# Gate matrix of a PEER layer: the last row of each group on ScalarE, three buffers, merge two groups behind

## The chip, the cores and the metric

The kernel runs on one core of a Trainium2 chip. The time is that of one execution on the device, in microseconds (us); lower is better. Three runs of the kernel before took 3328.36, 3329.63 and 3330.40 us.

## What is computed

Two blocks with 256 tokens of width 2048: first an S5 mixer and a sparse attention, then a HGRN2 and gated delta mixer followed by a PEER feed-forward layer. Only the PEER layer matters here. It has 16384 experts, written as pairs (i, j) of two indices of 128. Each token has 8 heads, and each head takes its 16 best experts, so a token has 128 entries (index i, index j, gate):

```python
best, pos = lax.top_k(cand, P_TOPK)
expert = i1[pos // P_TOPK] * N_KEYS + i2[pos % P_TOPK]
gate = jax.nn.softmax(best, axis=-1)
hid = gelu(x . u_tab[expert])
y = sum(gate * hid * v_tab[expert])
```

The kernel gathers nothing. It multiplies every token with all experts and weighs the result with a gate matrix that holds 0 for the experts that a token did not choose. For token t, that matrix is a 128 x 128 product of two matrices with one nonzero in each of the token's 128 entries: R (entry x first index, with the gate there) and C (entry x second index, with a 1 there): W[t] = R^T C.

## The kernel before

All weights stream through the core in pieces of 512 KB: SyncE issues the transfer into a ring of three raw slots; ScalarE rounds the piece into its high part (`high`, L231, 128x1024); VectorE subtracts to get the low part (`low`, L237, 128x1024); TensorE multiplies high and low parts (24 matmuls for a piece in `up_piece`, L2373). A slot comes free for the next transfer when its `low` is done.

The experts are 64 pairs of 256 (`up(j)`, four pieces of the first table, and `down(j)`, four pieces of the second, L2439). In `peer` the first LEAD = 16 `up`s come before the first `down`. Eleven of them (STORED) have their gelu put into the large tile `w` before the gates are known; five (HELD) are computed in the course of the gate loop and keep their gelu in PSUM banks 2, 3, 4, 5 and 0 (`HELD_BANK`). So the loop that makes the gate matrix also carries 20 pieces of `up`.

**The gate loop** goes over 64 groups of 4 tokens (`GATE_GROUPS`, `PER_GROUP`). Its engines run their own programs in order and meet at semaphores:

- VectorE, for group n: four rows (L2657, `tensor_scalar` is_equal and mult over the iota with the token's first index and gate as per-partition operands, 128x128 each); the four columns in one instruction (L2660, 128x512); `merge(n - 1)` (L2647, 128x88: the product's cells of the 11 stored pairs times the stored gelu); in 20 of the 64 groups (`early_slot`: 0, 4, 7, 10, 13, 16, 20 ... 61) one `low`. The rows and columns have two buffers, so that group n waits for the product of group n - 2.
- TensorE: in the 20 slots first one held piece (L2373, 24 matmuls), then `gates(n)` (L2414): four matmuls of 128x128 in fp32, each of which the profile shows as two records, into PSUM bank 6 or 7. It waits for the rows, the columns and `placed` of group n - 2.
- ScalarE: in the slots one `high` (L231), five times a gelu (L2485) too; then `place(n)` (L2492, 128x424: the other cells of the product, copied into `w`), which waits for `merged(n)`.
- SyncE: the piece transfers (L2335), each when a `low` is done.

After the loop TensorE runs `up(16)` and then `down(0)`. In `up(16)` (bank 16 % 3 = 1) it waits for `stored` only, and `down(0)` waits for all of the gates. VectorE multiplies the five held gelus with their gates (L2671), which waits for `placed(63)`. Then a loop over the rest of the pairs follows, in which VectorE also adds up the output (L2685).

`k.stepper(eng, sem)` gives a function that makes its engine wait for the completion of the instruction just issued; it is used where the next instruction reads the result.

Of the kernel before, what the change touches and what calls it, by code (L numbers as in the profile page):

```python
# [25 lines left out]
ACT = mybir.ActivationFunctionType  # L26
AX = mybir.AxisListType

P = 128
# [2176 lines left out]
WG, HN_LOW, YACC = 0, 32768, H3  # L2206
# [7 lines left out]
STORED = LEAD - HELD  # L2214
HELD_BANK = (2, 3, 4, 5, 0)
PER_GROUP = 4
GATE_GROUPS = T // PER_GROUP
E1T, E2T, GT = (YACC + T * i for i in range(3))
GROWS, GCOLS = YACC + 768, YACC + 1792

# [32 lines left out]
def peer(k):  # L2255


    nc, ps = k.nc, k.ps
# [11 lines left out]
    w, w_t = k.at(WG, 32768), k.at(WG, 32768).rearrange("p (i t) -> p t i", t=T)  # L2270
    y = k.at(YACC, 4096)
    e1t, e2t, gt = (k.at(o, T) for o in (E1T, E2T, GT))
    rows = [k.at(GROWS + 512 * b, 512) for b in range(2)]
    cols = [k.at(GCOLS + 512 * b, 512) for b in range(2)]
    gparts = [k.split_small(P + 256 * i - WORK0, 512, 512 * i) for i in range(2)]
    keys_in, copied, sums, raised, e_done, chosen, turned, e_out = (k.sem("pq_" + n) for n in (
        "keys copied sums raised exps chosen turned turned_out").split())
    rows_ready, cols_ready, product, placed, merged = (k.sem("gm_" + n) for n in (
        "rows_ready cols_ready product placed merged").split())
    stored, gelu_done, gated, g_high, g_low, y_full, y_free, reloaded = (k.sem("ex_" + n) for n in (  # L2280
        "stored gelu_done gated g_high g_low y_full y_free rows_reloaded").split())
    E0 = PIECES * AT_EXPERTS
# [11 lines left out]
    def u_piece(j, part):  # L2294

        return E0 + PIECES * (j if j < LEAD else 2 * j - LEAD) + part

    def v_piece(j, part):
        return E0 + PIECES * (LEAD + (2 * j + 1 if j < WITH_UP else WITH_UP + j)) + part
# [7 lines left out]
    def slot_of(j):  # L2307
        return w[:, j * 512:(j + 1) * 512]
# [12 lines left out]
    def early_slot(n):  # L2321


        count = PIECES * HELD
        return n * count // GATE_GROUPS != (n - 1) * count // GATE_GROUPS

    with nc.Block() as block:
# [24 lines left out]
        def _(pe):  # L2352
# [25 lines left out]
            def up(j, m, looped):  # L2378

                if j == LEAD and not looped:  # L2380
                    pe.wait_ge(stored, STORED)
                elif j >= LEAD:
                    pe.wait_ge(gated, m * BODY + (j - 2))
                elif j >= 3:
                    pe.wait_ge(stored, j - 2)
                for part in range(PIECES):
                    up_piece(u_piece(j, part), part, j % 3, m)
# [17 lines left out]
                mm.then_inc(turned, 1)  # L2405

            def gates(n):
                b = n % 2
                pe.wait_ge(rows_ready, n + 1)
                pe.wait_ge(cols_ready, n + 1)  # L2410
                if n >= 2:
                    pe.wait_ge(placed, n - 1)
                for j in range(PER_GROUP):
                    mm = nc.tensor.matmul(ps[:, 6 + b, j * P:(j + 1) * P], rows[b][:, j * P:(j + 1) * P],  # L2414
                                          cols[b][:, j * P:(j + 1) * P], start=True, stop=True)
                mm.then_inc(product, 1)

# [51 lines left out]

        @block.scalar  # L2470
        def _(act):
            early = iter(range(E0, E0 + PIECES * (LEAD + 1)))

            def high(n):
                for _, c in zip(range(n), early):
                    k.high(act, c)

            def copy(h):
                act.wait_ge(sums, h + 1)
                nc.scalar.copy(sc.rearrange("p (t n) -> p t n", t=TT)[:, :, h * 256:(h + 1) * 256],  # L2480
                               ps[:, 3 + h % 5, :].rearrange("p (t n) -> p t n", t=TT)).then_inc(copied, 1)

            def gelu(c, bank, m=0):
                act.wait_ge(k.multiplied, m * PER + (c + 1))
                nc.scalar.activation(ps[:, bank, :], ps[:, bank, :], ACT.Gelu).then_inc(gelu_done, 1)  # L2485

            def held_gelu(i):
                gelu(u_piece(STORED + i, PIECES - 1), HELD_BANK[i])

            def place(n):  # L2490
                act.wait_ge(merged, n + 1)
                nc.scalar.copy(w_t[:, n * PER_GROUP:(n + 1) * PER_GROUP, 2 * STORED:],  # L2492
                               ps[:, 6 + n % 2, :].rearrange("p (j i) -> p j i", i=P)[:, :, 2 * STORED:]
                               ).then_inc(placed, 1)

            def step(j, m, looped):

                if looped or 1 <= j <= WITH_UP:
                    gelu(u_piece(j + LEAD - 1, PIECES - 1), (j + LEAD - 1) % 3, m)
                act.wait_ge(gated, m * BODY + (j + 1))  # L2500
                if looped or j >= 2:

                    act.wait_ge(k.multiplied, m * PER + (v_piece(j - 2, PIECES - 1) + 1))
                nc.scalar.copy(gparts[j % 2][0], w[:, bass.ds(m * (512 * BODY) + j * 512, 512)]).then_inc(g_high, 1)
                if j < WITH_UP:
                    for part in range(PIECES):
                        k.high(act, v_piece(j, part), m, PER)
                if j < PAIRS - 1:
                    for part in range(PIECES):
                        k.high(act, v_piece(j, PIECES) + part, m, PER)  # L2510

            for c in range(PIECES * AT_WQ, PIECES * (AT_WQ + 1)):
                k.high(act, c)
            for h in range(PH):
                if h + 1 < PH:
                    for c in range(PIECES * (AT_WQ + h + 1), PIECES * (AT_WQ + h + 2)):
                        k.high(act, c)
                else:
                    high(PIECES)
                act.wait_ge(k.multiplied, PIECES * (AT_WQ + h + 1))  # L2520
                nc.scalar.copy(qry[:, h * BANK:(h + 1) * BANK], ps[:, (AT_WQ + h) % BANKS, :]).then_inc(k.bank_free, 1)
                if h:
                    copy(h - 1)
            for j in range(STORED):
                high(PIECES)
                act.wait_ge(k.multiplied, u_piece(j, PIECES - 1) + 1)
                nc.scalar.activation(slot_of(j), ps[:, j % 3, :], ACT.Gelu).then_inc(stored, 1)
                if j == 0:
                    copy(PH - 1)
                if j == 6:  # L2530
                    act.wait_ge(raised, 1)
                    nc.scalar.activation(gate, gate, ACT.Exp).then_inc(e_done, 1)
            piece = 0
            high(1)
            for n in range(GATE_GROUPS):
                if early_slot(n):
                    high(1)
                    if piece and piece % PIECES == 0:
                        held_gelu(piece // PIECES - 1)
                    piece += 1  # L2540
                place(n)
            held_gelu(HELD - 1)
            act.wait_ge(k.spilled, 16)
            act.dma_start(y, k.h3_rows).then_inc(reloaded, 16)
            run(act, step)

        @block.vector
        def _(dve):
            v = k.stepper(dve, k.vstep)
            tt_, ts_ = nc.vector.tensor_tensor, nc.vector.tensor_scalar  # L2550
            early = iter(range(E0, E0 + PIECES * (LEAD + 1)))

            def low(n):
                for _, c in zip(range(n), early):
                    k.low(dve, c)
# [88 lines left out]
            def merge(n):  # L2644
                dve.wait_ge(product, n + 1)
                cells = w_t[:, n * PER_GROUP:(n + 1) * PER_GROUP, 0:2 * STORED]
                tt_(cells, ps[:, 6 + n % 2, :].rearrange("p (j i) -> p j i", i=P)[:, :, 0:2 * STORED], cells,  # L2647
                    ALU.mult).then_inc(merged, 1)

            dve.wait_ge(stored, STORED)  # L2650
            for n in range(GATE_GROUPS):
                b = n % 2
                if n >= 2:
                    dve.wait_ge(product, n - 1)
                for j in range(PER_GROUP):
                    t = n * PER_GROUP + j
                    last = ts_(rows[b][:, j * P:(j + 1) * P], k.iota, e1t[:, t:t + 1], gt[:, t:t + 1],  # L2657
                               ALU.is_equal, ALU.mult)
                last.then_inc(rows_ready, 1)
                tt_(cols[b].rearrange("p (j i) -> p j i", i=P), k.iota.unsqueeze(1).to_broadcast([P, PER_GROUP, P]),  # L2660
                    e2t[:, n * PER_GROUP:(n + 1) * PER_GROUP].unsqueeze(2).to_broadcast([P, PER_GROUP, P]),
                    ALU.is_equal).then_inc(cols_ready, 1)
                if n:
                    merge(n - 1)
                if early_slot(n):
                    low(1)
            merge(GATE_GROUPS - 1)
            dve.wait_ge(placed, GATE_GROUPS)
            for i in range(HELD):
# [171 lines left out]
```

## Time and profile before

| | |
|---|---|
| runs | 3328.36, 3329.63, 3330.40 us |
| profiled execution, its own time | 3324.11 us |
| its span | 3322.3 us |
| TensorE busy | 3073.0 us (92%) |
| VectorE busy | 2201.1 us (66%) |
| ScalarE busy | 1431.5 us (43%) |
| GpSimd busy | 29.5 us (1%) |
| mean granted TensorE clock | 0.96 |

The profiled execution has its own time, and a span inside it (first to last instruction). Busy times are sums over the whole span and say nothing of a single stage; the stage of the gate loop has to be cut out by its times. PE is TensorE's matmuls and PEld its weight loads, which overlap; DVE is VectorE, ACT ScalarE. A row of the timeline has the start in us, the time to the end of the (merged) instructions, the engine and line, and in brackets how long the engine had been idle and what ended that. Durations include the latency to the last write; the next instruction of an engine often starts before that, so the distance of two starts (a "step") is what an instruction costs its engine.

### The profile page before, as it was taken

Reading aid. Unit: us, or ns where it says so; the run is one execution under the profiler, and the core shown is the slowest. Engines: PE = TensorE matmul, PEld = TensorE weight load, DVE = VectorE, ACT = ScalarE, POOL = GpSimd, SP = SyncE. Lnnn points to the kernel's source line nnn. Section 1 sums busy time; section 2 is a strip of 40 time slices with the busy share of each in tenths; the row PEclk is TensorE's granted clock in tenths of the full one; section 3 lists DMA queues with packets and bytes.
Section 4 is the critical chain, followed back from the end, with each engine's and each line's share of the span. In section 5 each row is a group of like instructions: output and inputs, shape, how many; then the busy total and the mean of one; then the engine's idle time right before and its main releaser. Section 6 shows DMA issues by size and latency. Waiting matters only on the chain. (4 is left out here: it accounts for less than half of the span.)

```text
span 3322.3 us, 60164 instructions
## 1 busy us (share of the span) xinstructions
PE 3073.0 (92%) x23855; PEld 2521.6 (76%) x23922; DVE 2201.1 (66%) x3106; ACT 1431.5 (43%) x1805; POOL 29.5 (1%) x32
## 2 busy tenths in 40 slices
PE   7787899999987789999979988999999999999997
PEld 6674799988886678998869877777777777777654
DVE  8765534555555675575549999777777777777654
ACT  4223434565652543363434445444444444444443
POOL 0000000000000020000000000000000000000000
PEclk9768899999998899999989999999999999999999
DMA  5214655544434433353645532655565655655664
GB/s 199 77 52 152 204 158 184 161 140 140 140 123 156 140 115 102 109 172 102 196 159 173 174 112 77 212 193 189 192 198 194 191 189 193 197 190 186 194 193 150
DMA packets 143950, 529.74 MB, mean 159 GB/s; under 512 B 16992, under 2 KB 17760, under 8 KB 142048
## 3 DMA queue, kind: packets, MB, share of 16 engines
q1 hardware_dynamic: 140400, 510.33, 47.5%
q10 hardware_dynamic: 3312, 15.92, 1.3%
q8 instruction: 189, 3.10, 0.4%
q14 instruction: 49, 0.40, 0.0%
HBM read 521.99 MB, written 4.19 MB: 158 GB/s over the span
## 5 line engine op out<-in xcount | busy, mean ns | idle before, releaser
L237 DVE TENSOR_TENSOR mem<-mem,rounded 128x1024 bf16<-128x1024 f32 x952 | 1155.2, 1227 | 759.4 <-ACT rounded L231 751.9
L231 ACT CAST rounded<-mem 128x1024 fp32r<-128x1024 f32 x952 | 993.4, 1047 | 1399.6 <-PE ps L264 337.2
L264 PE MATMUL ps<-rounded 128*128 128x256 f32 x3328 | 475.1, 292 | 49.8 <-DVE mem L237 42.5
L264 PEld LDWEIGHTS ps<-rounded 128*128 128x128 f32 x3328 | 423.4, 193 | 55.2 <-issue 24.7
L264 PE MATMUL ps<-rounded,mem 128*128 128x256 bf16 x3328 | 445.2, 279 | 0.0
L264 PE MATMUL ps<-mem,rounded 128*128 128x256 bf16 x3328 | 428.5, 276 | 13.7 <-DVE mem L237 13.7
L264 PEld LDWEIGHTS ps<-mem,rounded 128*128 128x128 bf16 x3328 | 319.3, 99 | 61.2 <-DVE mem L237 9.0
L264 PEld LDWEIGHTS ps<-rounded,mem 128*128 128x128 bf16 x3328 | 316.3, 98 | 61.7 <-issue 1.4
L2439 PE MATMUL ps<-rounded 128*128 128x512 f32 x1024 | 335.5, 441 | 2.7 <-DVE mem L2695 2.1
L2685 DVE TENSOR_TENSOR mem<-mem,ps 128x512 f32<-128x512 f32 x392 | 268.5, 685 | 66.9 <-PE ps L2439 60.0
L2439 PE MATMUL ps<-mem,rounded 128*128 128x512 bf16 x969 | 294.4, 381 | 3.7
L2373 PE MATMUL ps<-rounded 128*128 128x256 f32 x2048 | 287.7, 288 | 8.8 <-DVE mem L2692 2.4
L2373 PE MATMUL ps<-rounded,mem 128*128 128x256 bf16 x2048 | 275.8, 276 | 0.0
L2373 PEld LDWEIGHTS ps<-rounded 128*128 128x128 f32 x2048 | 259.2, 189 | 17.8 <-issue 8.0
L2439 PE MATMUL ps<-rounded,mem 128*128 128x512 bf16 x1016 | 271.1, 387 | 0.5
L2373 PE MATMUL ps<-mem,rounded 128*128 128x256 bf16 x2048 | 246.5, 272 | 1.6 <-DVE mem L237 1.6
L2439 PEld LDWEIGHTS ps<-rounded 128*128 128x128 f32 x1024 | 189.4, 189 | 58.2 <-DVE mem L2695 2.5
L2373 PEld LDWEIGHTS ps<-mem,rounded 128*128 128x128 bf16 x2048 | 199.6, 98 | 27.3 <-DVE mem L237 2.7
L2373 PEld LDWEIGHTS ps<-rounded,mem 128*128 128x128 bf16 x2048 | 186.7, 96 | 36.0
L2439 PEld LDWEIGHTS ps<-rounded,mem 128*128 128x128 bf16 x1024 | 98.9, 97 | 126.5
L2439 PEld LDWEIGHTS ps<-mem,rounded 128*128 128x128 bf16 x1024 | 78.8, 97 | 137.1 <-issue 70.8
L2414 PE MATMUL ps<-mem 128*128 128x128 f32 x512 | 72.1, 285 | 23.5 <-DVE mem L2660 21.7
(407 smaller groups left out, 2368.6 us busy)
## 6 DMA issues: line engine op xcount, KB each, us to landing
mem<-experts SPq DMA_DIRECT2D x512, 512.0 KB, 4.2
mem<-weights SPq DMA_DIRECT2D x440, 512.0 KB, 3.6
mem<-x_t SPq DMA_DIRECT2D x4, 512.0 KB, 9.9
mem<-x_rows SPq DMA_DIRECT2D x1, 2048.0 KB, 7.6
mem<-ln_g ACTq DMA_DIRECT2D x2, 1024.0 KB, 5.2
mem<-ln_b ACTq DMA_DIRECT2D x2, 1024.0 KB, 7.6
mem<-cmp_w_k ACTq DMA_DIRECT2D x4, 512.0 KB, 5.5
mem<-cmp_w_v ACTq DMA_DIRECT2D x4, 512.0 KB, 4.8
```

The source lines that it names most:

```text
L231: self.nc.scalar.copy(self.parts(c % SLOTS)[0], self.raw(c % RAW)).then_inc(self.high_done, 1)
L237: self.nc.vector.tensor_tensor(wl, self.raw(c % RAW), wh.bitcast(F32), ALU.subtract).then_inc(self.low_done, 1)
L264: mm = self.nc.tensor.matmul(self.ps[:, bank, half * 256:half * 256 + 256], a, b, start=(part == 0 and n == 0), stop=(part == PIECES - 1 a ...
L2373: mm = nc.tensor.matmul(ps[:, bank, half * T:half * T + T], a, b, start=(part == 0 and n == 0), stop=(part == PIECES - 1 and n == len(KIND ...
L2414: mm = nc.tensor.matmul(ps[:, 6 + b, j * P:(j + 1) * P], rows[b][:, j * P:(j + 1) * P], cols[b][:, j * P:(j + 1) * P], start=True, stop=True)
L2439: mm = nc.tensor.matmul(ps[:, bank, :], a, b, start=(j <= WITH_UP and half == 0 and i == 2 * tt), stop=((j < WITH_UP or j == PAIRS - 1) an ...
L2685: nc.vector.tensor_tensor(y[:, a:a + BANK], y[:, a:a + BANK], ps[:, bank, :], ALU.add).then_inc(y_free, 1)
```

## The change

`PER_GROUP - 1` rows of a group are still made by VectorE. The last row is made by ScalarE in two instructions, `row(n)`: dist = |e1[t] - iota| (Abs, the index as a per-partition bias), then relu(gate - 2 dist), which is the gate where dist is 0 and 0 elsewhere. The two are joined by a step wait. ScalarE makes the rows of groups 0 and 1 ahead of the loop, and `row(n + 2)` at the head of its group n, before that group's `high`, gelu and `place(n)`. Rows and columns have three buffers, and the product three banks (6, 7, 1), so that the waits for a buffer reach back three groups. VectorE merges group n - 2 in group n, and the last two groups after the loop. TensorE waits for `last_row` as well, and `up(16)`, which uses bank 1, waits for `placed` of 63 groups (that is for `place(62)`, the last user of bank 1).

```diff
--- before.py
+++ after.py
@@ -2216,7 +2216,8 @@
 PER_GROUP = 4
 GATE_GROUPS = T // PER_GROUP
 E1T, E2T, GT = (YACC + T * i for i in range(3))
-GROWS, GCOLS = YACC + 768, YACC + 1792
+GROWS, GCOLS, GDIST = YACC + 768, YACC + 2304, YACC + 3840
+GATE_BANK = (6, 7, 1)
 
 
 
@@ -2270,13 +2271,14 @@
     w, w_t = k.at(WG, 32768), k.at(WG, 32768).rearrange("p (i t) -> p t i", t=T)
     y = k.at(YACC, 4096)
     e1t, e2t, gt = (k.at(o, T) for o in (E1T, E2T, GT))
-    rows = [k.at(GROWS + 512 * b, 512) for b in range(2)]
-    cols = [k.at(GCOLS + 512 * b, 512) for b in range(2)]
+    rows = [k.at(GROWS + 512 * b, 512) for b in range(3)]
+    cols = [k.at(GCOLS + 512 * b, 512) for b in range(3)]
     gparts = [k.split_small(P + 256 * i - WORK0, 512, 512 * i) for i in range(2)]
     keys_in, copied, sums, raised, e_done, chosen, turned, e_out = (k.sem("pq_" + n) for n in (
         "keys copied sums raised exps chosen turned turned_out").split())
-    rows_ready, cols_ready, product, placed, merged = (k.sem("gm_" + n) for n in (
-        "rows_ready cols_ready product placed merged").split())
+    dist = [k.at(GDIST + P * b, P) for b in range(2)]
+    rows_ready, last_row, cols_ready, product, placed, merged = (k.sem("gm_" + n) for n in (
+        "rows_ready last_row_ready cols_ready product placed merged").split())
     stored, gelu_done, gated, g_high, g_low, y_full, y_free, reloaded = (k.sem("ex_" + n) for n in (
         "stored gelu_done gated g_high g_low y_full y_free rows_reloaded").split())
     E0 = PIECES * AT_EXPERTS
@@ -2378,7 +2380,7 @@
             def up(j, m, looped):
 
                 if j == LEAD and not looped:
-                    pe.wait_ge(stored, STORED)
+                    pe.wait_ge(placed, GATE_GROUPS - 1)
                 elif j >= LEAD:
                     pe.wait_ge(gated, m * BODY + (j - 2))
                 elif j >= 3:
@@ -2405,13 +2407,16 @@
                 mm.then_inc(turned, 1)
 
             def gates(n):
-                b = n % 2
+                b = n % 3
                 pe.wait_ge(rows_ready, n + 1)
+                pe.wait_ge(last_row, n + 1)
                 pe.wait_ge(cols_ready, n + 1)
-                if n >= 2:
-                    pe.wait_ge(placed, n - 1)
+                if n == 2:
+                    pe.wait_ge(stored, STORED)
+                if n >= 3:
+                    pe.wait_ge(placed, n - 2)
                 for j in range(PER_GROUP):
-                    mm = nc.tensor.matmul(ps[:, 6 + b, j * P:(j + 1) * P], rows[b][:, j * P:(j + 1) * P],
+                    mm = nc.tensor.matmul(ps[:, GATE_BANK[b], j * P:(j + 1) * P], rows[b][:, j * P:(j + 1) * P],
                                           cols[b][:, j * P:(j + 1) * P], start=True, stop=True)
                 mm.then_inc(product, 1)
 
@@ -2469,6 +2474,7 @@
 
         @block.scalar
         def _(act):
+            a = k.stepper(act, k.astep)
             early = iter(range(E0, E0 + PIECES * (LEAD + 1)))
 
             def high(n):
@@ -2487,10 +2493,22 @@
             def held_gelu(i):
                 gelu(u_piece(STORED + i, PIECES - 1), HELD_BANK[i])
 
+            def row(n):
+
+
+                b, t = n % 3, n * PER_GROUP + PER_GROUP - 1
+                if n == 0:
+                    act.wait_ge(e_out, 3)
+                if n >= 3:
+                    act.wait_ge(product, n - 2)
+                a(nc.scalar.activation(dist[n % 2], k.iota, ACT.Abs, bias=e1t[:, t:t + 1], scale=-1.0))
+                nc.scalar.activation(rows[b][:, PER_GROUP * P - P:], dist[n % 2], ACT.Relu, bias=gt[:, t:t + 1],
+                                     scale=-2.0).then_inc(last_row, 1)
+
             def place(n):
                 act.wait_ge(merged, n + 1)
                 nc.scalar.copy(w_t[:, n * PER_GROUP:(n + 1) * PER_GROUP, 2 * STORED:],
-                               ps[:, 6 + n % 2, :].rearrange("p (j i) -> p j i", i=P)[:, :, 2 * STORED:]
+                               ps[:, GATE_BANK[n % 3], :].rearrange("p (j i) -> p j i", i=P)[:, :, 2 * STORED:]
                                ).then_inc(placed, 1)
 
             def step(j, m, looped):
@@ -2532,7 +2550,11 @@
                     nc.scalar.activation(gate, gate, ACT.Exp).then_inc(e_done, 1)
             piece = 0
             high(1)
+            row(0)
+            row(1)
             for n in range(GATE_GROUPS):
+                if n + 2 < GATE_GROUPS:
+                    row(n + 2)
                 if early_slot(n):
                     high(1)
                     if piece and piece % PIECES == 0:
@@ -2644,15 +2666,15 @@
             def merge(n):
                 dve.wait_ge(product, n + 1)
                 cells = w_t[:, n * PER_GROUP:(n + 1) * PER_GROUP, 0:2 * STORED]
-                tt_(cells, ps[:, 6 + n % 2, :].rearrange("p (j i) -> p j i", i=P)[:, :, 0:2 * STORED], cells,
+                tt_(cells, ps[:, GATE_BANK[n % 3], :].rearrange("p (j i) -> p j i", i=P)[:, :, 0:2 * STORED], cells,
                     ALU.mult).then_inc(merged, 1)
 
             dve.wait_ge(stored, STORED)
             for n in range(GATE_GROUPS):
-                b = n % 2
-                if n >= 2:
-                    dve.wait_ge(product, n - 1)
-                for j in range(PER_GROUP):
+                b = n % 3
+                if n >= 3:
+                    dve.wait_ge(product, n - 2)
+                for j in range(PER_GROUP - 1):
                     t = n * PER_GROUP + j
                     last = ts_(rows[b][:, j * P:(j + 1) * P], k.iota, e1t[:, t:t + 1], gt[:, t:t + 1],
                                ALU.is_equal, ALU.mult)
@@ -2660,10 +2682,11 @@
                 tt_(cols[b].rearrange("p (j i) -> p j i", i=P), k.iota.unsqueeze(1).to_broadcast([P, PER_GROUP, P]),
                     e2t[:, n * PER_GROUP:(n + 1) * PER_GROUP].unsqueeze(2).to_broadcast([P, PER_GROUP, P]),
                     ALU.is_equal).then_inc(cols_ready, 1)
-                if n:
-                    merge(n - 1)
+                if n >= 2:
+                    merge(n - 2)
                 if early_slot(n):
                     low(1)
+            merge(GATE_GROUPS - 2)
             merge(GATE_GROUPS - 1)
             dve.wait_ge(placed, GATE_GROUPS)
             for i in range(HELD):
```

## Rows read from the trace of the kernel before

**Rows 1.** Busy time in stretches: the gate loop, the stretch behind it
```profile
core 0: us, PE busy (x) PEld busy (x) DVE busy (x) ACT busy (x) POOL busy (x), PEclk, DMA share, GB/s
1932.00:2079.00 147.00, 123.53 (x992) 111.44 (x990) 143.93 (x405) 76.44 (x89) 0.00 (x0) 0.99 0.23 77
...
2079.00:2200.00 121.00, 119.98 (x808) 88.21 (x812) 89.15 (x102) 54.24 (x59) 0.00 (x0) 1.00 0.64 209
```

**Rows 2.** Waits in the gate loop (1932 to 2079 us): total us, times, longest
```profile
ACT mem L2492 <- DVE mem L2647: 69.4, 64, 2.8
PEld ps L2414 <- DVE mem L2657: 25.8, 25, 1.8
```

**Rows 3.** Waits behind the loop, 2079 to 2200 us
```profile
PE ps L2439 <- DVE mem L2685: 0.6, 1, 0.6
```

**Rows 4.** Timeline of the loop: a group without and one with a piece
```profile
1946.09 1.11 DVE L2657 TENSOR_SCALAR mem<-mem 128x128 f32<-128x128 f32 x4
...
1947.12 0.68 DVE L2660 TENSOR_TENSOR mem<-mem 128x512 f32<-128x512 f32 x1
1947.72 0.32 DVE L2647 TENSOR_TENSOR mem<-ps,mem 128x88 f32<-128x88 f32 x1
1947.87 0.97 PEld L2414 LDWEIGHTS ps<-mem 128*128 128x128 f32 x8 [1.02 <-DVE mem L2657]
...
1947.94 1.11 DVE L2657 TENSOR_SCALAR mem<-mem 128x128 f32<-128x128 f32 x4
...
1948.76 1.02 PEld L2373 LDWEIGHTS ps<-rounded 128*128 128x128 f32 x8
...
1949.57 0.33 DVE L2647 TENSOR_TENSOR mem<-ps,mem 128x88 f32<-128x88 f32 x1
1949.81 1.22 DVE L237 TENSOR_TENSOR mem<-mem,rounded 128x1024 bf16<-128x1024 f32 x1
...
1950.95 1.12 DVE L2657 TENSOR_SCALAR mem<-mem 128x128 f32<-128x128 f32 x4
1951.51 0.97 PEld L2414 LDWEIGHTS ps<-mem 128*128 128x128 f32 x8
...
1952.71 0.33 DVE L2647 TENSOR_TENSOR mem<-ps,mem 128x88 f32<-128x88 f32 x1
```

**Rows 5.** Timeline of the loop: ScalarE in a slot with a gelu
```profile
1963.64 0.92 ACT L2492 COPY mem<-ps 128x424 f32<-128x424 f32 x1 [0.96 <-DVE mem L2647]
...
1964.35 1.07 ACT L231 CAST rounded<-mem 128x1024 fp32r<-128x1024 f32 x1
...
1965.31 0.60 ACT L2485 ACTIVATE ps<-ps 128x512 f32<-128x512 f32 x1
```

**Rows 6.** Timeline: start of the loop, VectorE's group 61, the loop's end
```profile
1932.31 1.11 DVE L2657 TENSOR_SCALAR mem<-mem 128x128 f32<-128x128 f32 x4
...
2069.92 1.11 DVE L2657 TENSOR_SCALAR mem<-mem 128x128 f32<-128x128 f32 x4
...
2077.60 1.20 PE L2373 MATMUL ps<-rounded 128*128 128x256 f32 x8
```

**Rows 7.** Groups of ScalarE instructions by form, 128x128: count, busy us, mean ns
```profile
L1230 ACT ACTIVATE mem<-ps,mem 128x128 f32<-128x128 f32 x96 | 28.2, 364 | 5.0 <-PE ps L1110 4.7
...
L1863 ACT ACTIVATE mem<-mem 128x128 f32<-128x128 f32 x32 | 9.9, 310 | 0.9
```

**Rows 8.** Timeline of ScalarE: two with a step wait between, three without
```profile
10.19 0.23 ACT L536 ACTIVATE mem<-mem 128x32 f32<-128x32 f32 x1
10.45 0.23 ACT L537 ACTIVATE mem<-mem 128x32 f32<-128x32 f32 x1
...
707.04 0.88 ACT L1230 ACTIVATE mem<-ps,mem 128x128 f32<-128x128 f32 x3
```

**Rows 9.** Groups of ScalarE: the table loads on the stored gelu's line
```profile
L2527 ACT ACT_TABLE_LOAD x2 | 2.6, 1283 | 0.0
```

**Rows 10.** Busy time in stretches of 5 us early in the loop, columns as rows 1
```profile
1935.00:1940.00 5.00, 3.37 (x17) 3.18 (x16) 4.62 (x16) 1.53 (x2) 0.00 (x0) 0.66 0.31 107
```

## The prediction

> **What bounds the kernel now.** The busy shares of the whole span don't answer this; the gate loop has to be read by itself. I first cut the span into stretches [rows 1]: in the 147 us of the loop VectorE is busy for 143.9 us, TensorE for 123.5, ScalarE for 76.4. So VectorE sets the pace. The waits of the same stretch [rows 2] say the same from the other side: ScalarE's `place` waits 69.4 us in all for VectorE's `merge`, TensorE's weight loads 25.8 us for VectorE's rows. Behind the loop TensorE is busy for 119.98 of 121 us [rows 1], and what it still waits for there is one 0.6 us behind VectorE [rows 3]. So whatever brings the start of `up(16)` forward brings the end forward by as much, and the whole question is when `up(16)` starts. Before, that is at 2077.60, 145.3 us after the loop's first row at 1932.31 [rows 6].
>
> **VectorE's group.** I count steps from start to start, not durations, since these overlap. A group without a piece goes from 1946.09 to 1947.94, that is 1.85 us: four rows 1.03 (0.257 each), the columns 0.60, the merge 0.22. A group with a piece goes from 1947.94 to 1950.95, 3.01 us, so a `low` adds 1.16 [rows 4]. 64 x 1.85 + 20 x 1.16 = 141.6 us. The first row of group 61, after 61 groups with 19 pieces, would be due after 61 x 1.85 + 19 x 1.16 - 0.22 (group 0 merges nothing) = 134.7 us; it comes after 137.6 (2069.92 - 1932.31) [rows 6]. The missing 2.9 us are waits of the merge for a product just made: behind a held piece `gates` starts at 1951.51, and the merge, due 0.60 after the columns, starts at 1952.71, 1.20 us after it [rows 4].
>
> **The row that moves** takes one step of 0.257 off each group: 1.593 us is left, 2.75 with a piece. **The merge two groups behind** asks for a product started over a group earlier, and the third buffer takes the other wait away; I cost both at nothing and take back the 2.9 us. Group 61 then starts after 61 x 1.593 + 19 x 1.16 - 0.45 (two groups merge nothing) = 118.8 us. That is 18.8 us earlier: 15.9 for the row, 2.9 for the waits. This holds if VectorE never waits, so the cover must be counted.
>
> **ScalarE's cover.** Its steps are 0.71 for `place`, 0.96 for `high`, at most 0.60 for a gelu [rows 5]. There is no row of an Abs or Relu with a per-partition bias from SBUF. The nearest are 128x128 with a per-partition operand, 0.364 us, and with none, 0.310 [rows 7]. Three in a row of the former take 0.88, a step of 0.257; a step wait cost 0.03 from end to start [rows 8]. I take the one with the operand: `row` costs 0.364 + 0.03 + 0.257 = 0.65 us of ScalarE and is ready 0.76 us after its start. The lower bound is 0.31 + 0.03 + 0.21 = 0.55; for the upper I take 0.95, by letting both instructions last 0.47 and the wait 0.12. The Trainium skill (ScalarE: Activation LUTs, What ACT_TABLE_LOAD costs) gives 280 ns + 0.833 ns per element with a pointer bias, 387 ns here, and by that `row` would cost about 0.71. Its queue matters too: `row(n + 2)` stands ahead of the group's `high` and `place(n)`, and behind `place(n - 1)`, which waits for a merge. Three groups with one piece are the tightest stretch: VectorE 3 x 1.593 + 1.16 = 5.94 us; ScalarE 3 x (0.71 + 0.65) + 0.96 = 5.04, or 5.64 with one of the five gelus. It fits, up to a `row` of 0.95 us. A late row delays only `gates`, whose product is asked for two groups later: after merge(n - 3) starts, `place` can start at 0.37, `row(n)` at 1.08, ready 1.84; the columns are ready at 0.22 + 0.77 + 0.69 = 1.68. So the product comes 0.16 us later than the columns would let it, against over 3 us of lag.
>
> **TensorE's cover.** A `gates` occupies it for 0.89 (1947.87 to 1948.76), a held piece with the next one for 2.75 (1948.76 to 1951.51) [rows 4]. Three groups with a piece: 5.42 of 5.94. Two `gates` in a row that wait for nothing are not in the trace; if the fourth wait or the pairing costs 0.35 between them, it is 5.42 + 2 x 0.35 = 6.1, and TensorE would be last by 0.2 per slot, 3 us in all. I take 0, since it goes from `gates` into the piece and back without a gap.
>
> **The new tail.** `up(16)` must now wait for `place(62)`. From the first row of group 61 (0): its `low` ends the group at 2.75, group 62 at 4.34, the columns of 63 are ready at 5.8, and TensorE's last `gates` runs from 5.9 to 6.8. ScalarE: merge(60) starts at 4.1, `place(60)` at 4.5, `row(63)` at 5.2, `high` at 5.85, `place(61)` at 6.8, `place(62)` at 7.5, complete at 8.45. `up(16)` starts at 8.45 instead of 7.68 (2077.60 - 2069.92): TensorE idles 1.6 us, and 0.8 us is given back. VectorE and ScalarE are ahead of TensorE by that, so the 0.6 us wait of [rows 3] may go; I count 0.3. Two things could add: the granted clock was 0.66 (part of it at 1.2 instead of 2.4 GHz) in a stretch that followed short waits of TensorE [rows 10]; if the 1.6 us bring that on once more, 5 us at 0.66 cost 1.7 us. The value taken is 0. SyncE's queue is not reordered: it still follows the lows, which come sooner by what VectorE gains. Before the loop, rows 0 to 2 cost ScalarE 2 us while it has nothing due but a `high`.
>
> **The sum:** 18.8 - 0.8 + 0.3 = 18.3 us. The profiled execution took 3324.1 us, which gives 3305.8; the median of the three runs is 5.5 us above it, 3329.6, and I forecast against that: 3311.3 us.
>
> **Rivals.**
> 1. A cover is short in part: `row` at 0.85 to 1.1 us, or `gates` in pairs dearer, so that one of the two is last in the slots. A `row` of 1.05 makes ScalarE's three groups 6.24 instead of 5.94, and the gelu slots 6.84; over 20 slots some 8 us. Gain 8 to 15 us, about 3318. For it: the slack is only 0.9 us in 5.94; against: the 69 us of idle time [rows 2].
> 2. ScalarE becomes as long as VectorE was, nothing gained, about 3328 to 3331. This needs a `row` of 1.1 to 1.3 us, nearly twice what rows 7 and 8 make of it.
> 3. Slower: the table. If Abs and Relu were not in gelu's table, each `row` would need loads of 1.283 us [rows 9], two in a group. ScalarE's loop is then 64 x (0.71 + 0.65 + 2.57) + 20 x 0.96 + 3 = 274 us instead of 145, the time about 3458. The mechanism decides from a `row` of about 1.2 us on, where ScalarE's 64 groups pass 145 us. Against it: the loop before mixes gelu, cast and copy without a load, and the two loads on the gelu's line lie outside it [rows 9]. That says nothing of Abs and Relu. The Trainium skill (ScalarE: Activation LUTs, Table sets: the hidden batching unit) says that relu, copy, identity and abs sit in every set; by that the price is 0. No trace here shows either function.
> 4. By VectorE's side: the same page (Rules for kernel authors) says to do relu, max, add and mul on VectorE, not on ScalarE. The rows agree on the price: 0.65 us there against 0.257 here. That alone would make it a loss; with VectorE last and ScalarE idle for 69.4 us [rows 2] it is none. If the row brought nothing and only the buffers counted, the gain would be 2.9 - 0.8, and the time 3327.5; this lies with rival 2.
>
> **How the numbers follow.** Forecast 0.71 (gain 15 to 21 us), rival 1 0.17, rivals 2 and 4 together 0.07, rival 3 and any other loss 0.05. A measurement of this kernel tells about 0.2%, 6.7 us, from no change: faster 0.89, same 0.06, slower 0.05. Low end: all bounds on the good side (cheaper tail, 0.6 us wait gone, a `merge` wait or two more) give 21 us, and 2 us of drift of the runs, 3306.5. High end: rival 1 down to a gain of 9 us, 3320.5.
>
> **What would show it.** Right: `row`'s two instructions at some 0.36 us; the loop's busy VectorE near 100% and its waits for products gone; three groups with a piece at 5.94 us; `up(16)` some 127 us after the first row, with a wait of 1.6 us before it that ends with `place(62)`; behind that, TensorE as busy as before. Wrong: table loads in the loop; VectorE waiting for products, with `gates` released by ScalarE; a loop shorter by 18 us with the end earlier by less.

## The result and the profile after

Six runs of the changed kernel took 3301.14 to 3307.31 us, median 3303.22, against 3329.39 of six runs of before, the three known ones among them: a ratio of 0.9925 (interval 0.9913 to 0.9937), faster by 26.2 us. I had forecast 3311.3, at the lowest 3306.5. The side was right, the range missed by 3.3 us. The profiled execution took 3305.53 us with a span of 3303.7, which is 18.6 us less than the profiled execution before; so already here the profile and the medians don't tell the same gain.

The gate loop and the stretch behind it in the changed kernel, busy time by engine, columns as in [rows 1]:
```profile
1935.00:2061.00 126.00, 117.77 (x984) 108.62 (x982) 125.09 (x339) 110.00 (x214) 0.00 (x0) 0.99 0.27 89
2063.00:2184.00 121.00, 120.59 (x812) 88.83 (x816) 89.73 (x102) 53.58 (x57) 0.00 (x0) 1.00 0.62 208
```
VectorE is still the bound (125.1 of 126 us), but ScalarE is now at 110 and TensorE at 118: the three are close together. The waits of the loop answer to [rows 2]:
```profile
ACT mem L2510 <- DVE mem L2669: 13.2, 16, 2.4
PE ps L2419 <- ACT mem L2505: 4.3, 14, 0.5
DVE mem L2669 <- PE ps L2419: 1.0, 1, 1.0
```
ScalarE's `place` waits 13.2 us for the merge instead of 69.4. TensorE's `gates` now waits 14 times for ScalarE's row, 0.3 us each: the late row of the prediction, which had 0.16. VectorE waits for a product once, after the last group. The timeline of three groups with one piece answers to [rows 4]:
```profile
2046.30 0.84 DVE L2679 TENSOR_SCALAR mem<-mem 128x128 f32<-128x128 f32 x3
...
2047.90 0.84 DVE L2679 TENSOR_SCALAR mem<-mem 128x128 f32<-128x128 f32 x3
...
2050.65 0.84 DVE L2679 TENSOR_SCALAR mem<-mem 128x128 f32<-128x128 f32 x3
...
2052.25 0.84 DVE L2679 TENSOR_SCALAR mem<-mem 128x128 f32<-128x128 f32 x3
```
A group takes 1.60, one with a piece 2.75, three with a piece 5.95; the steps said 1.593, 2.75 and 5.94. The start of the loop and its end answer to [rows 6]:
```profile
1934.91 0.86 DVE L2679 TENSOR_SCALAR mem<-mem 128x128 f32<-128x128 f32 x3
...
2053.85 0.84 DVE L2679 TENSOR_SCALAR mem<-mem 128x128 f32<-128x128 f32 x3
...
2061.56 1.22 PE L2375 MATMUL ps<-rounded 128*128 128x256 f32 x8 [0.51 <-ACT mem L2510]
```
Group 61 starts 118.9 us after the first row (118.8 forecast), `up(16)` 126.65 us after it (118.8 + 8.45 = 127.25 forecast, 145.3 before). ScalarE's groups in the loop, beside [rows 7]:
```profile
L2505 ACT ACTIVATE mem<-mem 128x128 f32<-128x128 f32 x64 | 25.7, 402 | 2.1
L2504 ACT ACTIVATE mem<-mem 128x128 f32<-128x128 f32 x64 | 24.9, 389 | 1.1 <-DVE mem L2664 1.1
L231 ACT CAST rounded<-mem 128x1024 fp32r<-128x1024 f32 x19 | 19.6, 1029 | 0.0
```
There is no table load among them.

So the loop gave what it was to give, and 7.6 of the 26.2 us are outside it. From here on I split every profile in three: **ahead** (to VectorE's first row), **loop** (to `up(16)`) and **behind** (to the end of the span). Before: 1932.3, 145.3, 1244.7. Changed: 1934.9, 126.7, 1242.1. Two theories: A, the gain is the loop's, and the rest is that runs of one program differ by more than I allowed for; B, the changed kernel saves some 7 us outside the loop too.

### The profile page after: what moved, and what is told of

Read it like the earlier page. It is cut to its first block and busy times, and to the rows that moved or that the text cites. A ratio compares the mean times of both kernels' runs of the same rounds, so it can differ in the third digit from the quotient of the medians.

```text
span 3303.7 us, 60290 instructions
## 1 busy us (share of the span) xinstructions
PE 3067.2 (93%) x23855; PEld 2517.0 (76%) x23922; DVE 2181.8 (66%) x3042; ACT 1466.8 (44%) x1933; POOL 29.8 (1%) x32
## 5 line engine op out<-in xcount | busy, mean ns | idle before, releaser
L2375 PEld LDWEIGHTS ps<-rounded 128*128 128x128 f32 x2048 | 259.9, 190 | 18.3 <-issue 6.4
L337 PE MATMUL ps<-mem 128*128 128x128 f32 x96 | 18.6, 384 | 72.0 <-DVE mem L422 50.2
```

The costliest lines, as they stand in the source:

```text
L337: mm = nc.tensor.transpose(ps[:, b, c * T + tt * P:c * T + tt * P + P], src[:, tt * D + kc * P:tt * D + kc * P + P], self.ident)
L2375: mm = nc.tensor.matmul(ps[:, bank, half * T:half * T + T], a, b, start=(part == 0 and n == 0), stop=(part == PIECES - 1 and n == len(KIND ...
```

## The experiments

**The kernel before as a copy of itself, and the changed kernel again** (no edit).

> The kernel before against itself, to see how far runs of one program differ. Theory A (the 26 us between the medians are the 18.6 us of the gate loop plus variation from run to run outside it): 0 +- 2 us between the medians, single runs spread over 5 us, and a new profile shows the loop at 145.3 us again (first row to up(16)) while the stretches ahead of the loop or behind it move by some us. Theory B (the code outside the loop runs faster in the changed kernel by about 7 us): 0 between the medians and the stretches outside the loop the same as in the first profile within 1 us.

> The changed kernel once more. Theory A: gain 18 to 22 us against the runs of this call, loop 126.6 us, the rest as in the kernel before within its spread. Theory B: gain 25 to 27 us, and the profile's stretch behind the loop (up(16) to the end) shorter than 1244.7 us by 4 or more.

The copy: 3323.76 us (median of 12), the runs of before measured beside it 3326.82 (29 runs, 3320.5 to 3335.4), ratio 0.9992 (0.9981 to 1.0003). Two medians of one program lie 3 us apart, and single runs 15; both are more than the 2 and 5 us that I had expected. The changed kernel: 3304.80, ratio 0.9933 (0.9916 to 0.9950), 19.0 us below the copy and 22.0 below before. Profiles, ahead / loop / behind: copy 1935.6 / 145.6 / 1240.7, changed 1933.4 / 126.7 / 1243.7. The loops repeat within 0.3 us; what moves is outside, by 4.0 us behind the loop between two executions of the kernel before, where theory B allowed 1.

**Only the buffers and the lag: all four rows on VectorE.**
```diff
-                pe.wait_ge(last_row, n + 1)
...
-            row(0)
-            row(1)
             for n in range(GATE_GROUPS):
-                if n + 2 < GATE_GROUPS:
-                    row(n + 2)
...
-                for j in range(PER_GROUP - 1):
+                for j in range(PER_GROUP):
```


> The change with all four rows on VectorE: only three buffers, three banks and the merge two groups behind are left. My steps give a loop of 145.3 - 2.9 + 0.8 = 143.2 us, a gain of 2 us by theory A. Theory B (extra time saved outside the loop comes with the new layout of banks and buffers): about 9 us.

3322.41 us, ratio 0.9988 (0.9978 to 0.9998); loop 142.9 us. The buffers alone are worth 2.4 us of loop: VectorE's group 61 starts 134.3 us after the first row instead of 137.6, since the waits of [rows 4] are gone, and `up(16)`, which now waits for `place(62)`, follows it after 8.59 us instead of 7.68.

**Only the row: ScalarE makes it, with two buffers and the merge one group behind.**
```diff
-GATE_BANK = (6, 7, 1)
+GATE_BANK = (6, 7)
...
-                if n + 2 < GATE_GROUPS:
-                    row(n + 2)
+                if n + 1 < GATE_GROUPS:
+                    row(n + 1)
...
-                if n >= 2:
-                    merge(n - 2)
+                if n:
+                    merge(n - 1)
```
(and the waits for a buffer back to two groups, and `up(16)` waiting for `stored`, as in the kernel before.)

> The row on ScalarE alone, with two buffers, two banks and the merge one group behind as before (row(n + 1) at the head of group n). VectorE's group is shorter by 0.257, 15.9 us in all, but behind a held piece the product comes 4.75 us after the group's first row and the merge is due at 4.12: 0.63 us of wait in each of 20 slots, 12.6 instead of 2.9. Gain 6 us, loop 139 us. If the buffers did not matter, 16 us, loop 129 us.

3320.07 us, ratio 0.9980 (0.9971 to 0.9990); loop 142.0 us. The waits in the loop and one slot of the timeline:
```profile
DVE mem L2666 <- PE ps L2417: 14.1, 19, 0.8
...
1981.73 0.33 DVE L2666 TENSOR_TENSOR mem<-ps,mem 128x88 f32<-128x88 f32 x1 [0.75 <-PE ps L2417]
```
Row and buffers do not add up: 3.3 us of loop by the row, 2.4 by the buffers, 18.6 by both. With one group of lag a shorter VectorE group only asks for the product earlier. The waits came where they were computed, but dearer: the group behind a piece takes VectorE 2.43 us or more instead of 1.60, 0.83 lost in each of 19 slots and 15.8 us in all, not 12.6, and that is why the loop is 3 us longer than my 139 (the list above counts idle time alone). In the slot shown the merge starts 4.96 us after the group's first row, not 4.75. The `gates` ahead of the piece had waited 0.48 us for ScalarE's row there and started 0.12 us after the group's first row, against 0.07 before it in [rows 4]; that pushes the piece and the `gates` behind it back by 0.19 of the missing 0.21. No run tests it alone.

By the medians these two experiments gained 4.4 and 6.8 us against before, and 1.4 and 3.7 against the copy; two baselines of one program that differ by 3 us cannot check a step of 2 or 3 us, so the sizes are read from the loop.

**ScalarE's row made dearer** (Abs and its step wait done twice).
```diff
                 a(nc.scalar.activation(dist[n % 2], k.iota, ACT.Abs, bias=e1t[:, t:t + 1], scale=-1.0))
+                a(nc.scalar.activation(dist[n % 2], k.iota, ACT.Abs, bias=e1t[:, t:t + 1], scale=-1.0))
```


> The changed kernel with ScalarE's Abs (and its step wait) done twice in each row; the second writes the same values, so the output is the same. This takes ScalarE's row from the measured 0.73 us to 1.16. If ScalarE's cover is as thin as I worked out (a row of 0.95 us is where it comes last), three groups with a piece take 3 x (0.70 + 1.16) + 0.96 = 6.54 us on ScalarE against 5.94 on VectorE, the loop 64 x 1.86 + 20 x 0.96 + 3 = 141 us, and the gain falls from 18.6 to 4 us. If ScalarE has much idle time left (13 us in the loop now), the loop stays under 130 us.

3319.81 us, ratio 0.9980 (0.9971 to 0.9989); loop 139.5 us, ScalarE busy for 120.9 us and VectorE for 116.1 of the loop's first 126. One slot on ScalarE, the row, the cast, `place` and the next row, without a gap:
```profile
2001.46 0.39 ACT L2504 ACTIVATE mem<-mem 128x128 f32<-128x128 f32 x1
2001.88 0.40 ACT L2505 ACTIVATE mem<-mem 128x128 f32<-128x128 f32 x1
2002.31 0.40 ACT L2506 ACTIVATE mem<-mem 128x128 f32<-128x128 f32 x1
2002.62 1.03 ACT L231 CAST rounded<-mem 128x1024 fp32r<-128x1024 f32 x1
2003.56 0.94 ACT L2511 COPY mem<-ps 128x424 f32<-128x424 f32 x1
2004.29 0.38 ACT L2504 ACTIVATE mem<-mem 128x128 f32<-128x128 f32 x1
```
0.43 us more in each row take 12.8 of the 18.6 us away; 14 to 15 were expected. So the cover ends before a row of 1.16 us, and rival 1 was one short instruction away. Where between 0.73 and 1.16 it ends was not measured.

**The order of the three banks.**
```diff
-GATE_BANK = (6, 7, 1)
+GATE_BANK = (6, 1, 7)
...
-                    pe.wait_ge(placed, GATE_GROUPS - 1)
+                    pe.wait_ge(placed, GATE_GROUPS - 2)
...
-                if n == 2:
+                if n == 1:
                     pe.wait_ge(stored, STORED)
```


> The changed kernel with the banks in the order 6, 1, 7, so that the last group in bank 1 is 61 and up(16) waits for 62 placed groups, not 63. One place step less (0.71 us) before up(16): it starts with the end of the last gates. Loop 126.0 us instead of 126.7, the time 0.7 us below the changed kernel's, less than the runs differ by. If the wait in front of up(16) were covered by something else, 126.7.

Loop 125.9 us, and `up(16)` follows the last `gates` without a wait:
```profile
2061.36 1.21 PE L2375 MATMUL ps<-rounded 128*128 128x256 f32 x8
```
The median is 3306.96 us, the changed kernel's beside it 3307.36. The 0.7 us are seen in the loop and are too small for the medians. By the loop it is the best version.

**Copy and changed kernel a second and third time.**

> The kernel before against itself a second time. The first time its own median was 3.1 us below that of the runs of before in the same call, and the changed kernel was 19.0 us below this copy and 22.0 below the runs of before. Theory A (the gain is the 18.6 us of the loop; what goes beyond is the spread of the runs of before): copy and before within 3 us of each other, the changed kernel 17 to 21 us below the copy; ahead + behind the loop again 3176 to 3178 us in the profile. Theory B (7 us outside the loop): the changed kernel 25 us below the copy.

> The changed kernel a third time. Theory A: 17 to 21 us below the copy of before in this call, loop 126.7 us, ahead + behind 3176 to 3178 us. Theory B: 25 us below the copy.

Copy 3326.84 us, ratio 1.0003 (0.9994 to 1.0012), before 3326.19 (23 runs); changed 3307.36, ratio 0.9939 (0.9928 to 0.9951), 19.5 below the copy and 18.8 below before. Profiles: 1933.3 / 144.8 / 1242.7 and 1934.7 / 126.6 / 1244.8. For theory A, though ahead and behind add up to 3179.5 us in the changed kernel, where 3176 to 3178 was expected.

**Further profiled executions of before and of the changed kernel,** to catch a long one in the profiler.

> A further profile of the kernel before. Over 82 runs its median is 3326.6 us, over 18 runs that of the changed kernel 3305.2, 21.4 apart, while the loop explains 18.7 and the three profiled executions of before all lie at 3320.8 to 3322.3 us of span. Theory A (spread outside the loop): an execution with a span above 3325 us has its loop at 145.3 +- 0.5 us all the same, and the excess lies ahead of it or behind it, in waits for transfers. Theory C (the loop itself sometimes takes longer in the kernel before, since its product comes just in time for the merge): the excess lies in the loop, 147 us or more.

> The same as the look before it: a span above 3325 us with the loop at 145.3 +- 0.5 us speaks for theory A, one with the loop at 147 us or more for theory C.

> The same as the two looks before it: a span above 3325 us with the loop at 145.3 +- 0.5 us speaks for theory A, one with the loop at 147 us or more for theory C.

> A further profile of the changed kernel, to have four of it: loop 126.7 +- 0.2 us, a span of 3300 to 3306 us that varies with the stretches outside the loop (theory A), not with the loop.

> Before once more. In six profiles of before the stretch behind the loop took 1240.7 to 1248.8 us (mean 1245.4), with 9 waits of 1.6 to 2.5 us at heads of the rounds (issue or VectorE's gate product), in four of the changed kernel 1242.1 to 1244.8 (mean 1243.4), with one. Theory A (chance, the two kernels are alike there): this profile lies anywhere in 1240 to 1249. Theory D (the changed loop leaves VectorE and ScalarE further ahead, and that spares such waits): 1245 or more, with one or more of them.

> As the look before it: theory A anywhere in 1240 to 1249 us behind the loop, theory D 1245 or more with one or more waits of 1.6 to 2.5 us.

> The changed kernel: theory A anywhere in 1240 to 1249 us behind the loop, theory D 1244 or less with none or one wait of 1.6 to 2.5 us. Loop 126.7 us in both.

> As the look before it: theory A anywhere in 1240 to 1249 us behind the loop, theory D 1244 or less with none or one such wait. Loop 126.7 us in both.

Behind the gate loop the pairs run in a loop that the engines count in registers (the register loop), six pairs to a round; I call the start of a round its head. All profiles of the two programs (us; "heads" is the number of waits of TensorE of 1.5 us or more at these heads):

| profile | span | ahead | loop | behind | heads |
|---|---|---|---|---|---|
| before | 3322.3 | 1932.3 | 145.3 | 1244.7 | 1 |
| null_before | 3321.9 | 1935.6 | 145.6 | 1240.7 | 0 |
| null_before_b | 3320.8 | 1933.3 | 144.8 | 1242.7 | 1 |
| null_look_1 | 3328.5 | 1934.8 | 144.9 | 1248.8 | 2 |
| null_look_2 | 3330.8 | 1937.5 | 144.9 | 1248.4 | 3 |
| null_look_3 | 3323.6 | 1931.5 | 144.8 | 1247.3 | 2 |
| null_look_4 | 3324.8 | 1933.2 | 144.8 | 1246.8 | 1 |
| null_look_5 | 3325.5 | 1931.5 | 145.3 | 1248.7 | 3 |
| changed | 3303.7 | 1934.9 | 126.7 | 1242.1 | 0 |
| after_again | 3303.8 | 1933.4 | 126.7 | 1243.7 | 0 |
| after_third | 3306.2 | 1934.7 | 126.6 | 1244.8 | 1 |
| after_look | 3302.8 | 1933.0 | 126.7 | 1243.1 | 0 |
| after_look_2 | 3307.5 | 1934.5 | 126.7 | 1246.4 | 0 |
| after_look_3 | 3302.1 | 1932.8 | 126.7 | 1242.7 | 0 |

The two long executions of before (spans 3328.5 and 3330.8) have the same loop as the others: theory C falls. Theory A's "waits for transfers" did not come either: the long waits at the heads are put down to VectorE's product or to nothing. Means: ahead 1933.7 before and 1933.9 changed, loop 145.05 and 126.65, behind 1246.0 and 1243.8. So the gain in the profiles is 18.4 in the loop, -0.2 ahead, 2.2 behind. A head where TensorE loses time, in the longest execution of before (`null_look_2`), ScalarE and TensorE:
```profile
2608.62 0.58 ACT L2485 ACTIVATE ps<-ps 128x512 f32<-128x512 f32 x1 [4.37 <-PE ps L2439]
...
2610.54 1.22 PE L2373 MATMUL ps<-rounded 128*128 128x256 f32 x8 [1.95 <-DVE mem L2692]
```
and one where it hardly does, in the changed kernel, TensorE and VectorE:
```profile
2586.64 1.22 PE L2375 MATMUL ps<-rounded 128*128 128x256 f32 x8 [0.17 <-issue]
2587.25 0.69 DVE L2715 TENSOR_TENSOR mem<-ps,mem 128x512 f32 x1
```
ScalarE stands still for 4.37 us at the head in both. TensorE comes back 1.95 us late in one and 0.17 us late in the other. The product named as releaser is not what it waits for: in the second trace TensorE starts before that product, as the code allows (`up` asks for `gated` of two pairs earlier).

The table's differences behind the loop can be taken apart. A round takes 130.8 us plus TensorE's wait at its end: the waits at the seven heads add up to 4.2 us on average before and 2.9 changed. What follows the last head takes either 323.3 to 323.4 or 324.9 to 325.0 us, the longer in five of eight executions of before and in two of six changed. It is the granted clock: at the exit of the register loop TensorE waits 2.06 or 2.07 us in all fourteen. Over the 10 us behind that wait the clock is 1.00 in eight of them (`after` for one) and 0.83 in six, here in `after_again`, columns as in [rows 1]:
```profile
3112.00:3122.00 10.00, 9.77 (x37) 5.20 (x38) 4.96 (x5) 2.63 (x4) 0.00 (x0) 0.83 0.50 157
```
That is part of the time at 1.2 instead of 2.4 GHz, and it costs 1.6 us, in both kernels. The seventh long one is `null_look_5`, whose clock falls behind the 1.93 us wait at the last head.

Is the 2.2 us an effect of the change? Thirteen long waits at heads in eight executions of before stand against one in six of the changed kernel, and theory D's counts came in all four of the last profiles, but the one of `after_look_2` took 1246.4 us without such a wait, against D's 1244 or less. All four lie in theory A's 1240 to 1249. The single executions spread by 8 us, so that 2.2 +- 2.7 is what 8 and 6 of them can tell. Where copy and changed kernel were profiled side by side on one chip, behind was longer in the changed kernel (1243.7 and 1244.8 against 1240.7 and 1242.7); on the two chips of the last eight profiles it was shorter (1243.1, 1246.4 and 1242.7 against 1246.8 to 1248.8). And `rows_vector`, `row_only` and `abs_twice`, whose loops take 142.9, 142.0 and 139.5 us, have 1244.3, 1242.5 and 1243.7 behind, with one, no and one long wait: a short gate loop is not what it needs. The effect is not shown.

**ScalarE's additional code in the kernel before.**
```diff
+            def spare_row(n):
+                t = n * PER_GROUP + PER_GROUP - 1
+                if n == 0:
+                    act.wait_ge(e_out, 3)
+                a(nc.scalar.activation(dist[0], k.iota, ACT.Abs, bias=e1t[:, t:t + 1], scale=-1.0))
+                a(nc.scalar.activation(dist[1], dist[0], ACT.Relu, bias=gt[:, t:t + 1], scale=-2.0),
+                  spare_done if n == GATE_GROUPS - 1 else None)
...
+                spare_row(n)
                 place(n)
```


> The kernel before, whose ScalarE also makes an Abs and a Relu of 128x128 in every group, into a spare place that nobody reads: VectorE still makes all four rows. It has ScalarE's 128 additional instructions of the changed kernel, so that its code behind the loop lies where the changed kernel has it, without the shorter loop. ScalarE idles 69.4 us in that loop, and the pair costs it 0.86 us per group, 55 us: the loop stays at 145 to 147 us. Theory D1 (the place of ScalarE's code spares the waits at the heads of the rounds): behind the loop 1244 us or less, none or one wait of 1.6 us or more, and a median 1 to 3 us below before's less what the loop costs. Theory D2 (it has another cause, or is chance): behind the loop as in before, 1246 us on average with 1.6 such waits per execution, and the median at before's or above.

3326.32 us, ratio 0.9994 (0.9985 to 1.0003); profile 1931.9 / 145.8 / 1253.4 with four such waits at heads. The profile speaks against D1: with ScalarE's additional code the waits at heads are there all the same. But it is one execution, the longest of its eleven (3333.06 us, the others 3321.7 to 3328.4), and the median, 0.8 us below before's, lies where D1 had it (1 to 3 us below, less what the loop costs) rather than D2. So D1 is made unlikely, not ruled out, and what sets the waits at the heads stays open; moving the code of TensorE or VectorE alone was not tried.

## Why the prediction was right or wrong

**The bound.** Right. VectorE sets the loop's pace before and after, and behind the loop TensorE is busy for 120.6 of 121 us.

**VectorE's group, 15.9 + 2.9 us.** Right: 118.9 us to group 61 against 118.8. The 2.9 us of waits are gone; by themselves the buffers give 3.3 at group 61 and 2.4 at `up(16)`. What I did not write is that the two parts need each other: without the lag the row brings 3.3 us, not 15.9.

**ScalarE's cover.** Held, with less left over. I took 0.364 us for an instruction with an operand per partition, the row nearest, and 0.65 for the row; it is 0.389 and 0.402, and a row is 0.73 (`abs_twice` shows the step of 0.42 to 0.43 and 0.31 after the last). The Trainium skill's price (ScalarE: Activation LUTs, What ACT_TABLE_LOAD costs) comes to an estimate of 387 ns and was the closer one: the trace agrees within 15 ns. Three groups with a piece then take 3 x 1.44 + 0.96 = 5.28 of 5.94 us.

**TensorE's cover.** Right: three `gates` in a row run as `x24`, and the next instruction starts at 2043.29, 2.68 us after them: 0.89 each, so pairs cost nothing extra.
```profile
2040.61 2.85 PE L2419 MATMUL ps<-mem 128*128 128x128 f32 x24
```

**The tail, -0.8 us.** Wrong in size. I put `up(16)` 8.45 us after group 61's first row; it came after 7.71, with 0.5 us of idle time, not 1.6. I had a `high` on ScalarE in group 61. The code has 68 pieces to split in that stage, one was already split ahead of the loop, and the last slot finds none left: 19 casts in the loop's profile, not 20. The kernel before has 19 casts to 20 `low`s in its loop too, so its trace could have told me. Without the 0.96 us `up(16)` would come at 7.49, and the loop's share of the sum is 18.8 + 0.2 = 19.0; measured are 18.65 between the first two profiles and 18.4 between the means. The 0.6 us by which `up(16)` came ahead of my 127.25 are this one error of 0.74 in the tail; group 61 was right to 0.1. No fall of the clock came with the short wait: it is 1.00 in the 121 us behind.

**The table (rival 3) and the dearer engine (rival 4).** No load came, and ScalarE's row, at 0.73 us against 0.257 on VectorE, pays because VectorE was last. The Trainium skill says that relu and abs sit in every set (ScalarE: Activation LUTs, Table sets: the hidden batching unit); the trace agrees for gelu's, with no table load among 64 rows and the gelus between them.

**The step that failed** is a term of the low end, "and 2 us of drift of the runs", together with the base of 3329.6. I took the spread from three runs that happened to lie within 2.04 us. Over 104 runs of before and its copies the times go from 3317.5 to 3335.4, median 3326.9; over 21 runs of the changed kernel from 3301.1 to 3309.3, median 3304.9. The mechanism of the gate loop held; what lay outside my range is made up as follows. From 3311.3 to 3303.2 are 8.1 us. The base was 2.7 too high (3329.6 for 3326.9). Six runs gave 1.7 less than all 21 (3303.2 for 3304.9). The gain was 3.7 above my 18.3: 0.4 of it in the loop (18.4 for 18.0), 1.9 behind it (2.2 for 0.3), -0.2 ahead, and 1.6 that the profiles do not show.

The first gain, 26.2 us, was luck on both sides: of draws of six from the 104 runs some 6% have a median as high as 3329.4, and of draws of six from the 21 some 3% one as low as 3303.2. The gain between all medians is 22.0 us (19.8 to 23.1 when the runs are drawn again at random), 0.66%. In the two series that ran on one and the same chip, with 76 runs of before and copies against 12 of the changed kernel, it is 20.5 (18.6 to 22.3), with my 18.3 just below. The 18.4 us of the loop are shown, the rest is not. My own text held the warning: the profiled execution lay 5.5 us below the three runs. The sum drawn from it, 3305.8, would have been within 0.9 us of 3304.9, which again takes luck, as that execution lay below the median of 3326.9 too.

## What to carry to other kernels

Count steps from start to start on the engine that is last, and lay the other engines' steps for the tightest stretch beside it: here this gave VectorE's 61 groups to 0.1 us of 119. A shorter group needs a longer lag in the same change: each alone gave less than a fifth of what both gave. Cut a list of waits with the loop's own ends, and compare steps as well, since waits are listed as idle time alone. And take the range from the spread of many runs of the same program, not from three of them.

## What the runs showed of the hardware that was not expected

Executions of one program differ by 18 us (3317.5 to 3335.4, 104 runs), 0.5%. In the eight that were profiled (spans 3320.8 to 3330.8) it is all outside the 145 us of the gate loop, which repeats within 0.8 us. At the head of each round of the register loop behind it, 7 times in an execution, ScalarE stands still for 4.2 to 4.4 us (30.5 us in all in `null_look_5`, 30.6 in the changed kernel's `after_look_3`). TensorE comes back 0 to 1.0 us late at most heads and 1.6 to 2.6 us late at some, not the same in two executions of one program; why is open. Over the 10 us behind one and the same wait of 2.06 to 2.07 us at the exit of that loop, the granted clock was 1.00 in eight of fourteen executions and 0.83 in six, which cost 1.6 us.
